# The state-space stage of a hybrid decoder step: its operand built by transfers during attention, its scan in halves, y and turns block by block

## The reference

```python
def s5_mix(u, s0_re, s0_im, a_re, a_im, log_dt, b_re, b_im, c_re, c_im, d_skip, w_glu, b_glu):
    ug = u.reshape(bsz, l, 32, 16)                      # 32 groups of 16 channels
    ab_re, ab_im, bb_re, bb_im = s5_discretize(...)
    bu_re = einsum('blgc,gpc->blgp', ug, bb_re)         # 64 complex states a group
    bu_im = einsum('blgc,gpc->blgp', ug, bb_im)
    p_re, p_im, s_re, s_im = associative_scan(_complex_affine_combine, (a_r, a_i, bu_re, bu_im), axis=1)
    ...                                                 # the 8 samples start from s0
    y = einsum('blgp,gcp->blgc', s_re, c_re) - einsum('blgp,gcp->blgc', s_im, c_im)
    g = gelu(y.reshape(bsz, l, 512) + d_skip * u)
    out = g * sigmoid(g @ w_glu + b_glu)
    return out, s_re[:, -1], s_im[:, -1]

def sb_weights(z, q_pos, k_pos):                        # sample rows: 8192 past keys, 8 heads
    log_keep = where(mask, log_sigmoid(-z), 0.0)
    after = cumsum(log_keep, reverse=True) - log_keep
    return where(mask, exp(log_sigmoid(z) + after), 0.0)
# o = weights @ v_past: the past values lie in pages of 128 positions, found through page_table

mixed = concatenate([rmsnorm(o_sb, g_sb_out), rmsnorm(o_ssm, g_ssm_out)])
```

## Times and profile before

| what | value |
|---|---|
| median of 3 runs | 2935.62 us (2934.2 to 2935.93) |
| profiled execution, its own time | 2925.83 us |
| its span | 2924.1 us |
| mean granted TensorE clock | 0.957 |
| PE busy | 2717.6 us, 93% of the span |
| DVE, ACT, POOL busy | 63%, 27%, 12% |
| the state-space stage | 1447.7 to 1653.7, 206.0 us, 7% of the span |
| DMA | 478.19 MB, mean 164 GB/s |

### The profile page before, as it was taken

How to read it: one execution, slowest core, us unless ns; L and a number is a source line. 1 busy time by engine, 2 the same in 40 slices (tenths; PEclk the granted TensorE clock), 3 DMA queues, 4 the chain that set the end, 5 groups by cost and what they waited for, 6 DMA issues and landing times. The chain is left out here.

```text
span 2924.1 us, 44166 instructions
## 1 busy us (share of the span) xinstructions
PE 2717.6 (93%) x15387; PEld 2195.3 (75%) x15387; DVE 1838.5 (63%) x2530; ACT 803.8 (27%) x1460; POOL 352.3 (12%) x581
## 2 busy tenths in 40 slices
PE   6789899999999999988879789988989999999998
PEld 4457666666666667865525789973989999999998
DVE  6559999899898937867552462564264444444445
ACT  4231211211111213049712541331051111111115
POOL 1010032322322211200122000031000000000000
PEclk7789999999999999999979799998999999999999
DMA  9876699989999835521197431144111111111111
GB/s 354 298 258 202 190 336 320 341 296 315 330 317 317 310 98 176 165 63 30 58 289 250 153 122 36 37 146 160 55 42 46 43 50 43 50 43 43 43 57 60
DMA packets 334116, 478.19 MB, mean 164 GB/s; under 512 B 26600, under 2 KB 215397, under 8 KB 332110
## 3 DMA queue, kind: packets, MB, share of 16 engines
q1 hardware_dynamic: 291110, 333.29, 34.5%
q0 software_dynamic: 42416, 142.32, 14.2%
q10 hardware_dynamic: 408, 0.31, 0.0%
HBM read 453.22 MB, written 22.62 MB: 163 GB/s over the span
## 5 line engine op out<-in xcount | busy, mean ns | idle before, releaser
L84 ACT ACTIVATE whi<-raw 128x1024 fp32r<-128x1024 f32 (+1 forms) x184 | 189.7, 1044 | 924.3 <-PE banks L113 807.7
L111 PE MATMUL banks<-ffn_hhi,whi 128*128 128x344 f32 x1056 | 339.9, 322 | 8.0 <-DVE ffn_hlo L141 5.1
L112 PE MATMUL banks<-ffn_hlo,whi 128*128 128x344 f32 x1056 | 338.6, 321 | 0.0
L113 PE MATMUL banks<-ffn_hhi,wlo 128*128 128x344 f32 x1056 | 338.6, 321 | 0.0
L111 PE MATMUL banks<-ffn_ghi,whi 128*128 128x344 f32 (+1 forms) x880 | 315.7, 359 | 10.8 <-DVE xT L1771 5.3
L113 PE MATMUL banks<-ffn_ghi,wlo 128*128 128x344 f32 (+1 forms) x880 | 310.8, 353 | 0.0
L112 PE MATMUL banks<-ffn_glo,whi 128*128 128x344 f32 (+1 forms) x880 | 309.8, 352 | 0.0
L88 DVE TENSOR_TENSOR wlo<-raw,whi 128x1024 fp32r<-128x1024 f32 (+1 forms) x184 | 222.5, 1215 | 134.7 <-ACT whi L84 134.4
L111 PE MATMUL banks<-a_hhi,whi 128*128 128x512 f32 x704 | 287.9, 409 | 6.9 <-DVE wlo L88 6.1
L624 DVE TENSOR_TENSOR ffn_kt<-ffn_kt,ffn_q 128x1024 f32<-128x1024 f32 x224 | 272.9, 1219 | 28.2 <-DMA ffn_kt<-in_cache_k_dram 28.2
L611 POOL DMA_DIRECT2D ffn_vt<-in_cache_v_dram x384 | 206.7, 538 | 654.4 <-issue 648.7
(11 more groups left out here) (474 smaller groups left out, 4762.8 us busy)
## 6 DMA issues: line engine op xcount, KB each, us to landing
ffn_kt<-in_cache_k_dram SPq DMA_DIRECT2D x448, 256.0 KB, 4.3
ffn_vt<-in_cache_v_dram POOLq DMA_DIRECT2D x384, 256.0 KB, 5.0
raw<-in_w_ffn_gate_dram SPq DMA_DIRECT2D x44, 512.0 KB, 4.5
raw<-in_w_ffn_up_dram SPq DMA_DIRECT2D x44, 512.0 KB, 4.1
raw<-in_w_ffn_down_dram SPq DMA_DIRECT2D x44, 512.0 KB, 4.6
last_kt<-in_cache_k_dram POOLq DMA_DIRECT2D x64, 256.0 KB, 3.1
s_vt<-in_cache_v_dram POOLq DMA_DIRECT2D x64, 256.0 KB, 5.1
s_vt<-in_cache_v_dram SPq DMA_DIRECT2D x64, 256.0 KB, 4.8
```

What stands on the lines that cost most here:

```text
L84: act.activation(self.k.whi[c % W_RING][:, 0:self.width], self.slots[s][:, 0:self.width], ACT.Copy).then_inc(self.hi_done, 1)
L111: pe.matmul(out, whi, rhi, start=first, stop=False)
L112: pe.matmul(out, whi, rlo, start=False, stop=False)
L113: return pe.matmul(out, wlo, rhi, start=False, stop=last)
```

## The change

X is no longer made by PE. During attention SP copies it together inside SBUF with 64 transfers of 16x4x128 numbers and 16 transfers of 16x32 single numbers for the samples, queued ahead of the stores of k and v; for that `project_in` writes the state-space rows of the projection de-interleaved (position l of each chunk together). POOL clears the 40 columns of samples in attention. The last sample's scores stay in SBUF, and its weights are made at the start of the stage. The ring of pages is 8 instead of 16, since X takes the place. The chain of DVE runs in two halves of 8 tiles, 18 steps each, on 128x1024 elements. PE's order is written anew: the value steps go between y quads, turns, and samples, and the turns of block i follow soon on its y quad. The norm of `oT`: sums behind y 4 and y 5 and, for the third tile, beside the gate's first unit; its sharpening and its products on DVE run beside the gate's first three units. The gate's weights 0 and 1 are loaded early.

```diff
-        self.z = at("last_z", [P, 512], 16)
+        self.z = at("last_z", [P, 512], 25)
...
+    def pe(self, pe):
+        sums, within = (self.k.ps[b] for b in self.banks)
         pe.wait_ge(self.softplus_done, 1)
-        pe.matmul(self.k.ps[self.bank], self.k.ones[:, :], self.e[:, :], start=True, stop=True).then_inc(self.sums, 1)
-
-    def within_page(self, pe):
+        pe.matmul(sums, self.k.ones[:, :], self.e[:, :], start=True, stop=True).then_inc(self.sums, 1)
         pe.wait_ge(self.consts, 2)
-        pe.wait_ge(self.later, 9)
-        pe.matmul(self.k.ps[self.bank], self.tri[:, :], self.e[:, :], start=True, stop=True).then_inc(self.within, 1)
+        pe.matmul(within, self.tri[:, :], self.e[:, :], start=True, stop=True).then_inc(self.within, 1)
...
-    VR = 16
+    VR = 8
...
-                    v.tensor_tensor(self.qkvu[:, n, t0:t0 + size], self.ps[bank][:, 0:size], late.inverse_rms(t),
-                                    ALU.mult).then_inc(proj.drained, 1)
+                    out, in_, root = self.qkvu[:, n, t0:t0 + size], self.ps[bank][:, 0:size], late.inverse_rms(t)
+                    if n >= 12:
+                        out = self.qkvu[:, n].rearrange("p (l j) -> p j l", l=8)[:, t0 // 8:(t0 + size) // 8]
+                        in_, root = (x.rearrange("p (j l) -> p j l", l=8) for x in (in_, root))
+                    v.tensor_tensor(out, in_, root, ALU.mult).then_inc(proj.drained, 1)
...
-                sp.dma_start(self.z_dram, self.last.z[:, :]).then_inc(self.z_kept, 16)
+                for l in range(8):
+                    for g in range(8):
+                        sp.dma_start(self.X[16 * l:16 * l + 16, g:32:8, 0:P],
+                                     self.qkvu[16 * g:16 * g + 16, 12:16, l * P:(l + 1) * P]).then_inc(self.x_built, 16)
+                sp.wait_ge(self.x_cleared, 1)
+                for l, at in ((0, P), (7, P + 32)):
+                    for b in range(NS):
+                        sp.dma_start(self.X[16 * l:16 * l + 16, :, at + b],
+                                     self.us_dram[b].rearrange("(g c) -> c g", c=16),
+                                     allow_slow_non_contiguous=True).then_inc(self.x_built, 16)
...
+                pool.memset(self.X[:, :, P:], 0.0).then_inc(self.x_cleared, 1)
...
-        U = place("s_U", [P, G, L, C], 16)
-        Us = place("s_Us", [40, G, L, C], 32)
+        S = place("s_S", [P, 2, T, SW], 32.5)
...
+        t = [place("s_t0", [P, T, P], 16.25), place("s_t1", [P, T, P], 24.25),
+             place("s_t2", [P, T, P], 0, ring=True), place("s_t3", [P, T, P], 8, ring=True)]
...
+        late_v = Values(self, place("s_vt", [P, Values.VR, 512], 16, ring=True), vw, in_x("s_vown", [P, Values.COUNT, 512], 25),
...
+        order = [("gsum", i) for i in range(T)] + [("y", i) for i in range(4)] + [("final", 0)]
+        order += [("turn", i) for i in range(4)] + [("ysample", i) for i in range(8)]
+        order += [("y", 4), ("y", 5), ("turn", 4), ("turn", 5), ("y", 6), ("y", 7), ("turn", 6), ("turn", 7), ("turn", 8)]
...
+                last.load_bias(sp)
+                late_v.load_pages(sp)
+                sp.dma_start(smalls[:, :], self.smalls_dram).then_inc(q["smalls_in"], 16)
                 for i in range(2):
                     sp.dma_start(rot[i][:, :, :].rearrange("p t n -> p (t n)"), self.rot_dram[i]).then_inc(q["rot_in"], 16)
-                sp.dma_start(smalls[:, :], self.smalls_dram).then_inc(q["smalls_in"], 16)
-                last.load_bias(sp)
+                late_v.load_weights(sp)
...
+                late_v.load(sp, 1, others[0:4 * L])
+                sp.wait_ge(q["v"], SCANNED[1])
+                for n in range(2):
+                    glu.w.load(sp, n, n, glu.src(n, n, 0), 4)
...
+                last.act(act)
+                for i in range(10):
+                    gsum(i)
+                last.weights(act)
+                for i in range(10, T):
+                    gsum(i)
+                for i in range(4):
+                    y(i)
...
+                split(3)
+                act.wait_ge(q["taken"], number["turn", 8] + 1)
+                act.activation(ghi[:, :, NP:NT], gT[:, :, NP:NT], ACT.Copy).then_inc(q["split_hi"], 1)
+                glu.w.hi(act, 2, 2, 2)
+                self.first_half.squares(act, 2)
+                for t_ in range(2):
+                    self.first_half.roots(act, t_)
+                for b_ in range(Values.COUNT):
+                    late_v.store(act, b_)
+                self.first_half.roots(act, 2)
...
+                for h, half in enumerate(halves):
+                    v.wait_ge(q["taken"], number["gsum", half.stop - 1] + 1)
+                    states(half)
...
+                v.wait_ge(q["split_hi"], 5)
+                v.wait_ge(q["taken"], number["y", 7] + 1)
...
+                self.first_half.adds(v, 2)
+
+                def scale(t_):
+                    t0, n = self.first_half.tiles[t_]
+                    self.first_half.invert(v, t_)
+                    for k in range(4):
+                        x = self.oT[:, k, t0:t0 + n]
+                        v.tensor_tensor(x, x, self.first_half.inverse_rms(t_), ALU.mult).then_inc(q["scaled"], 1)
...
+                def beside(n):
+                    if n < 3:
+                        scale(n)
+                glu.dve(v, gated, ahead=False, beside=beside)
...
+                pe.wait_ge(self.x_built, 16 * 80)
+                pe.wait_ge(q["gm_in"], 32)
+                last.pe(pe)
+                for t_ in range(T):
+                    gsum(t_)
+                weigh(5)
+                pe.wait_ge(q["toep_in"], 16 * L)
+                pe.wait_ge(q["ck_in"], 32)
+                pe.wait_ge(q["v"], SCANNED[0])
+                for i in range(4):
+                    y("y", i)
+                    weigh(1)
+                weigh(3)
...
+                for i in (4, 5):
+                    y("y", i)
+                    weigh(2)
+                    self.first_half.sums(pe, i - 4)
+                for i in (4, 5):
+                    turned(i)
+                    weigh(2)
+                for i in range(Values.COUNT * 16):
+                    weigh(1)
+                for i in (6, 7):
+                    y("y", i)
+                for b_ in range(Values.COUNT):
+                    late_v.columns(pe, b_)
+                for i in (6, 7):
+                    turned(i)
+                b = bank(("turn", 8))
                 for m in range(4):
                     ins = turn(b[:, m * NS:(m + 1) * NS], ys[:, m * P:(m + 1) * P], self.ident[0:NS, 0:NS])
-                done(ins)
-                pe.wait_ge(q["taken"], kinds["turn"] + 9)
-                glu.pe(pe)
+                ins.then_inc(q["quad"], 1)
+                pe.wait_ge(q["taken"], number["turn", 8] + 1)
+                pe.wait_ge(self.first_half.averaged, 2)
+
+                def beside(n):
+                    if n == 0:
+                        pe.wait_ge(late_v.stored, 1)
+                        self.first_half.sums(pe, 2)
+                glu.pe(pe, beside)
```

More of the change, by code:

```diff
@@ L2468, in ssm @@
-        for kind, n in (("U", 8), ("X", 11), ("gsum", 16), ("final", 1), ("y", 8), ("ysample", 8), ("turn", 9)):
-            kinds[kind] = quads
-            quads += n
+        halves = [slice(0, HT), slice(HT, T)]
+        SCANNED = (18, 36)
+        STATES = 46
         with nc.Block() as block:
@@ new lines, in turned, with split @@
+                def turned(i):
+                    m, half = divmod(i, 2)
+                    out = gT[:, m, 0:NP].rearrange("p (j l) -> p l j", l=L)[:, 4 * half:4 * half + 4]
+                    act.activation(out, bank(("turn", i)).rearrange("p (l j) -> p l j", l=4), ACT.Copy).then_inc(q["taken"], 1)
+                def split(m):
+                    act.wait_ge(q["taken"], number["turn", 2 * m + 1] + 1)
+                    act.activation(ghi[:, m, 0:NP], gT[:, m, 0:NP], ACT.Copy).then_inc(q["split_hi"], 1)
@@ new lines, in _ @@
+                for i in range(4):
+                    turned(i)
+                for i in range(8):
+                    b = bank(("ysample", i))[0:NS].rearrange("p (g n) -> p g n", g=4)[:, :, 0:C]
+                    act.activation(ys[:, :].rearrange("p (g c) -> p g c", c=C)[:, groups_of(i)], b,
+                                   ACT.Gelu_apprx_tanh).then_inc(q["taken"], 1)
+                for m in range(2):
+                    split(m)
+                for i in (4, 5):
+                    y(i)
+                    for t_ in range(i - 4, i - 3):
+                        self.first_half.squares(act, t_)
@@ new lines, in turned @@
+                def turned(i):
+                    m, half = divmod(i, 2)
+                    b = bank(("turn", i))
+                    pe.wait_ge(q["taken"], number["y", 2 * m + 1] + 1)
+                    for n in range(4):
+                        ins = turn(b[:, n * P:(n + 1) * P], yg[:, 4 * half + n, m * P:(m + 1) * P], self.ident[:, :])
```

(4 more changed lines are left out.)

359 lines of the change are left out of this document (142 added, 217 removed).

## The result

The change made the kernel slower: 2972.94 us (2968.53 to 2981.44, 4 runs) against 2934.91 us, 38 us between the medians, and a ratio of 1.0147 with a 95% interval of 1.0115 to 1.0179, by which it is 43 us. The forecast was 2940.2, its range ended at 2956.

What follows compares the result with a forecast made beforehand. The prediction held PE or DVE and the transfers each nearly full up to 1599.4. Attention +1.0, last value +0.1, columns -0.1, gate start +0.4 and gate +3.3 gave +4.6: 2930.4 profiled, 2940.2 as median; range 2918 to 2956.

Steps and rivals of the forecast that it cites:

- the ring of 8 taking back what the start gives: State-space stage: the smaller ring uses up the earlier start, so the last value is weighed at 1600 where it was 1599.9.
- Start, y 0 at 52.7: Stage's start: the first y matmul comes at 1499, bound by 13.2 MB of transfers wanted ahead of it.
- y 0 to 3 at 5.18 each with a step: First four y quads on PE: a quad of 4.22 plus a value step of 0.96 each, 20.7 us in all.
- Value steps at 3.3: Value steps paced by the ring of 8: 6.0 to 6.9 us for two steps, taken as 6.6, 3.3 a step.
- rival C: Paced phase: longer landings make a step 3.9 us, total 2950.4; with y 4 to 7 at 1.2 GHz 2956.7; chance 0.28.
- Samples at 11: Middle of the stage: eight ysample quads on PE at 1.37 each, 11 us, ending at 1552.
- y 4 and 5 with four steps at 15: Behind the samples: two y quads with four value steps take 15 us, ending at 1567.
- y 6 and 7 at 10.6: Behind the last value step: two y quads take 10.6 us, between 8.4 at full clock and 12.7 at 1.2 GHz.
- the slow case: Part of the slower rival: y 4 to y 7 all run at 1.2 GHz, +6.3 us, for a total of 2956.7.
- Gate start 16.9 behind the columns: Tail: PE's gate waits for two means of the norm on ACT, starting at 1627.5, +0.4 us.
- The norm's products exposed by 3.3: Gate: the norm's sharpening and products on DVE delay its first three units by 3.3 us, of 0 to 10.2.
- Rival D: Attention: X unfinished or k's stores late, since 16 single-number transfers issue slowly, so ACT waits; +20, 2960; chance 0.05.

Runs made afterwards that it cites:

- e2: The changed kernel with 13 extra matmuls, results unused, between the first five value steps ahead of y 0: stage 239.1 us against 258.0, ratio to before 1.0074.
- e1: The kernel before the change with a ring of 8 pages instead of 16, nothing else: stage 243.0 us against 214.6, ratio to before 1.0081.
- e3: The changed kernel with the norm's third squares and adds and two roots moved ahead of the last two y quads: stage 258.6 us, ratio to before 1.0108.
- e7: The changed kernel with ring of 12, early roots, nothing of y, samples or turns behind the last value step, and extra matmuls: stage 210.6 us, ratio to before 0.9988.
- e4: The changed kernel with its ring grown from 8 to 12 pages from the 33rd page on: stage 235.3 us against 258.0, ratio to before 1.0058.

## Why the prediction was wrong

The mechanism that I placed first, the ring of 8 taking back what the start gives, is there, and the start itself was right. Two terms were far off: the price of y 0 to 3, and that of a value step. By the forecast's own steps, from attention to the columns (forecast 164.3, measured 205.9, +41.6):

- **Start, y 0 at 52.7: measured 55.1 (+2.4).** gsum began at 19.2 against 18.2. The bytes bound y 0 as worked out.
- **y 0 to 3 at 5.18 each with a step: measured 9.37 (+16.8).** This is the step that failed most. I took 4.22 from the y phase before, where the clock was 1.00, without asking what had raised it. In the trace of before it was 0.66 in the window ahead, and rose as PE ran the two products with `s_le` and eight pages of values without a break, 1542.87 to 1549.06. The change moves these two products to the stage's start and leaves single steps with page waits in their place. I priced their removal at nothing, and weighed the clock only for y 4 to 7. e2 shows the price by putting 504-column work ahead of y 0: 16.7 us. e1 agrees with this account: with the small ring, but with these two products in place, the y phase had 1.00. The changed kernel with the products put back was not run, and its clock had risen once more and was lost in the wait of 3.45 us, as the windows above show.
- **Value steps at 3.3: measured 4.15 in the last ten (+8.5), and +6.1 in the seven behind y 3.** This is the second step that failed, +14.6 in all. The ring was right, the loop's terms too small. Landings were short, 3.5 us, nearer the best of the earlier trace rows than rival C had them:

```profile
s_vt<-in_cache_v_dram SPq DMA_DIRECT2D x8, 256.0 KB, 3.5
s_vt<-in_cache_v_dram POOLq DMA_DIRECT2D x8, 256.0 KB, 3.6
```

  That is for 1630 to 1650. The timelines of POOL and PE there show the rest of the loop:

```profile
1640.48 0.54 POOL L900 DMA_DIRECT2D s_vt<-in_cache_v_dram  x1 [1.92 <-issue]
1641.63 0.54 POOL L900 DMA_DIRECT2D s_vt<-in_cache_v_dram  x1 [0.61 <-issue]
1644.39 0.54 POOL L900 DMA_DIRECT2D s_vt<-in_cache_v_dram  x1 [2.22 <-issue]
```

```profile
1641.89 1.29 PE L911 MATMUL banks<-s_vt,s_vw 128*32 128x512 f32 x4 [0.77 <-DMA s_vt<-in_cache_v_dram]
1644.16 1.05 PE L911 MATMUL banks<-s_vt,s_vw 128*32 128x512 f32 x4 [0.97 <-DMA s_vt<-in_cache_v_dram]
1645.56 1.05 PE L911 MATMUL banks<-s_vt,s_vw 128*32 128x512 f32 x4 [0.35 <-DMA s_vt<-in_cache_v_dram]
1647.59 1.05 PE L911 MATMUL banks<-s_vt,s_vw 128*32 128x512 f32 x4 [0.98 <-DMA s_vt<-in_cache_v_dram]
```

  From a step's end (1643.18) to the next issue (1644.39) pass 1.2, and between two issues of a queue 1.2. A step's last two pages take 1.05 and not the 0.5 that I had: each pair starts at its own landing, and two pages alone take as long as a whole step in one piece, 1.07 in the trace of before. So 1.2 + 1.2 + 3.6 + 1.05 = 7.0 for two steps at full clock, 3.5 a step, where I had 6.6 and 3.3. That is an estimate from these rows, and the step shown took 3.9 from issue to issue. More was lost where the clock was low (2.16 was the longest such pair) or a turn waited for ACT, but 3.5 to 4.15 is not worked out step by step. C's time was nearer than mine, by another mechanism: it had 4.8 for the landing. (In e1, also with a ring of 8, a page took 4.2 to 4.5 to land in the y phase, and the step was 4.2 there too.)
- **Samples at 11: 15.5 with two steps (+4.5); y 4 and 5 with four steps at 15: 20.5 (+5.5).** Most of the samples' excess is the two value steps between them, 1.93 each: the sum has 8 x 1.37 and nothing for these. The sample quads themselves saw the same fall of the clock before the change (0.67 and 0.68), where 1.37 comes from. The clock's main part is behind them. Before the change no y quad followed on that fall; now y 4 did, and took 7.5 for it.
- **y 6 and 7 at 10.6: 8.4 (-2.2).** The Trainium skill's rule in "TensorE: Matmul & The Clock Gate", section "HAM oscillation — how this bites in real kernels", that bursts between transfer waits bring the clock down each time, stood behind the slow case. Here the stretch with waits had 0.84 and ended at 1.00, while 37.5 us without any wait stood at 0.50. In e3 it ended at 0.50. So in these runs waits of up to 2.5 us made the clock uncertain, and did not fix it low; the wait of 3.45 ahead of y 0 did bring it down. The slow case was also priced too low, at up to 12.7, "as part of a y is not clock-bound": at 0.50 y 6 and 7 took 15.0 in e3 and 8.4 at 1.00.
- **Gate start 16.9 behind the columns: 15.4.** Right, with its chain: the same waits in the same order.
- **The norm's products exposed by 3.3: 2.3.** The last gated product came 3.5 behind the gate's last matmul where it was 1.2. Right in kind.
- **Attention +1.0: +1.0** (167.6 from its first clearing to its last matmul against 166.6), a clearing of 1.17. Rival D is out: the 16 transfers of single numbers took 0.59 to issue each. The de-interleaved writes show no cost: from `a_proj` to attention pass 1112.1 against 1111.3.
- **After the stage**, a loss I had not counted: the memory stage's first turns run at the low clock, 3.65 instead of 1.94 us.
- **Readings and sums that don't come out.** 348 GB/s and a share of 0.97 hold for 1575 to 1590; the whole y phase had 295 and 0.87. The terms of the sum come to +4.7 and not +4.6. The 9.8 us between median and profiled execution are where one execution happened to lie: after the change the profiled one lies 8.5 above the median. None of the three decides anything here.

Rival C gave 2950 and 2957 with slow y 4 to 7; it named both causes, the ring and the clock, but had y 0 to 3 at full speed too. The measured 2972.94 lies beyond even its slow case. The range left out the case that came, because the clock entered it as a side effect on four quads and not as a term of its own on all of them.

## What to carry to other kernels

A duration taken from a trace holds at the clock of its row: when an edit moves work away from ahead of a long run of small products, or puts a wait there, look at what raised the clock there, and price the run at the lower level until something else raises it. A ring's worth is a loop, free to issue to landing to last use, divided by its depth: halving it cost 28 us in a kernel that was otherwise untouched, and four pages more, put where a dead tensor lay, gave 23 back. And losses that are visible in one trace can be bought back one by one and then together: here that brought the kernel level with the one before, not ahead of it. It does not tell what the rest of the change is worth, since of the three edits the extra matmuls and the early roots are new work and a new order, and the ring is still smaller than before.

## What the runs showed of the hardware

- TensorE stood at 1.2 GHz for 37.5 us in which it was never idle (y 0 to 3), and the same instructions ran at 2.4 GHz in e2 for 20.8 us. In the trace of before it also stood at 0.50 for 19.8 us with PE busy 19.3 (X quads, 1456.0 to 1475.8). It rose there while PE ran gsum quads (at 1479), the products with `s_le` and value steps (at 1547), and the 128x128 turns behind the columns (at 1619).
- In all ten profiled kernels the clock fell while PE ran the samples' 16-column products and the steps between them, with PE busy throughout (windows of 0.67 before and 0.68 after the change). In e7 it fell within y 5, 2.0 us after a wait of 1.45.
- Two pages weighed alone take PE 1.05 us, four in one piece 1.07.
- In the changed kernel, ring of 8, a page lands in 3.5 us at 1630 to 1650, and the core gets 251 GB/s in the last ten steps; in e1, ring of 8, in 4.2 to 4.5 at 249 GB/s in the y phase; with 12 in e4 in 5.0 to 5.2 at 327 GB/s.
- 64 transfers of 32 KB inside SBUF were issued at 0.66 us each beside attention, and ACT asked for the first store 24.7 us after the last was issued; attention was longer by the clearing alone.
